# Retention mixer: the sample output in a bank of its own, the sequence steps from the gate units on, and twenty matmuls of the output projection in the last head's tail

## What is computed

```python
def _retention_mixer(h, s0, pos0, w_in, gn_g, w_out):
    p = h @ w_in                                    # q, k (4 heads x 256), v, gate (4 heads x 512)
    q = _rotary(q, pos0);  k = _rotary(k, pos0) * (RET_DK ** -0.5)
    o, s = _retention_chunked(q, k, v, s0)          # per chunk of 128 tokens and head:
    #   att = (q k^T) * decay;  o = att v + (q * q_dec) s;  s = s * s_dec + (k * k_dec)^T v
    o = (o - mu) * lax.rsqrt(var + LN_EPS) * gn_g   # over the 512 values of a head
    o = o.reshape(B, L, RET_VW) * jax.nn.silu(gate)
    return o @ w_out, s

x = _layer_norm(ALPHA * x + (1.0 + gate_m) * y, ln_g[i, 0], ln_b[i, 0])
h = x * (1.0 + scale_f) + shift_f                   # goes to the router and the experts
```

## Time and profile before

| | |
|---|---|
| time, median of 3 runs | 2185.55 us |
| lowest and highest | 2180.12 and 2189.08 us |
| profiled execution: its own time | 2183.24 us |
| profiled execution: span in the trace | 2181.0 us |
| PE busy | 1841.5 us, 84% of the span |
| PE weight loads | 981.8 us |
| DVE, ACT, POOL busy | 788.5, 378.7, 347.4 us |
| `retention`, first to last matmul | 45.5 to 611.5 us |
| `mixer_end` of layer 0, first matmul | 612.15 us |

### The profile page before, as it was taken

The page is one execution under the profiler, slowest core; times in us unless marked ns, Lnnn a source line. Parts: engine busy times, 40 slices in busy tenths (PEclk is TensorE's granted clock), DMA queues, the critical chain, the costliest instruction groups (busy, mean ns, idle before and its releaser), DMA issues. The chain is left out here.

```text
span 2181.0 us, 36947 instructions
## 1 busy us (share of the span) xinstructions
PE 1841.5 (84%) x15665; PEld 981.8 (45%) x15665; DVE 788.5 (36%) x1650; ACT 378.7 (17%) x832; POOL 347.4 (16%) x456
## 2 busy tenths in 40 slices
PE   4999999999799769957979989988987779949970
PEld 3444444444334433324555665755754544433320
DVE  0123223223432320025764555555545423240107
ACT  1000000000000011114332242232232110001212
POOL 0011110101102200022521022031031002120103
PEclk9999999999989879978998989999998789959995
DMA  9364738556260199968431034034033584078964
GB/s 342 125 235 171 262 125 298 191 181 232 98 222 39 69 388 400 397 267 267 130 94 46 11 110 123 12 103 117 18 128 103 181 266 138 20 261 298 401 239 179
DMA packets 235089, 397.44 MB, mean 182 GB/s; under 512 B 17677, under 2 KB 91381, under 8 KB 234870
## 3 DMA queue, kind: packets, MB, share of 16 engines
q1 hardware_dynamic: 228974, 373.58, 49.1%
q0 software_dynamic: 5952, 21.50, 2.6%
HBM read 301.53 MB, written 93.51 MB: 181 GB/s over the span
## 5 line engine op out<-in xcount | busy, mean ns | idle before, releaser
L583 PE MATMUL bank<-ring,hT 128*128 128x512 f32 x768 | 349.7, 607 | 4.1 <-PEq L282 2.2
L583 PEld LDWEIGHTS bank<-ring,hT 128*128 128x128 f32 x768 | 144.7, 193 | 189.1 <-issue 188.9
L1235 PE MATMUL bank<-hT,ring 128*128 128x272 f32 x768 | 218.1, 419 | 0.0
L2385 PE MATMUL bank<-expert_w,exp_xT 128*32 128x512 f32 x1152 | 179.2, 630 | 13.2 <-DMA expert_w<-in_moe_w_gu_dram 9.1
L1235 PEld LDWEIGHTS bank<-hT,ring 128*128 128x128 f32 x768 | 141.2, 197 | 32.8 <-issue 8.0
L3095 PE MATMUL bank<-ring,oT 128*128 128x512 f32 x336 | 151.6, 613 | 0.7 <-PEq L484 0.7
L1229 PE MATMUL bank<-ring,hT 128*128 128x512 f32 x256 | 129.4, 636 | 0.0
L2385 PEld LDWEIGHTS bank<-expert_w,exp_xT 128*32 128x32 f32 x1152 | 48.0, 115 | 125.3 <-issue 120.1
L3095 PEld LDWEIGHTS bank<-ring,oT 128*128 128x128 f32 x336 | 65.6, 196 | 82.6 <-issue 82.6
L2409 PE MATMUL bank<-expert_w,exp_aT 128*32 128x512 f32 x576 | 89.5, 613 | 10.7 <-DMA expert_w<-in_moe_w_down_dram 9.3
L1905 DVE SCALAR_TENSOR_TENSOR dn_y<-dn_pre,dn_conv,dn_y 128x568 f32<-128x568 f32 x96 | 91.1, 949 | 3.4
(11 more groups left out here) (499 smaller groups left out, 2609.8 us busy)
## 6 DMA issues: line engine op xcount, KB each, us to landing
ring<-in_w_ada_dram SPq DMA_DIRECT2D x24, 2048.0 KB, 9.3
expert_w<-in_moe_w_gu_dram SPq DMA_DIRECT2D x24, 2048.0 KB, 15.5
expert_outputs<-ret_zeros SPq DMA_DIRECT2D x15, 2048.0 KB, 9.9
expert_w<-in_moe_w_down_dram SPq DMA_DIRECT2D x24, 1024.0 KB, 16.7
ring<-in_ret_w_in_dram SPq DMA_DIRECT2D x8, 2048.0 KB, 13.8
ret_Ss<-in_state_ret_dram SPq DMA_DIRECT2D x32, 512.0 KB, 5.2
out_dram<-ret_Ss SPq DMA_DIRECT2D x32, 512.0 KB, 4.2
oT<-in_moe_w_gu_dram SPq DMA_DIRECT2D x8, 2048.0 KB, 20.7
```

The lines of the kernel that those rows point to most:

```text
L583: last = pe.matmul(ps[u % 2][:, :], core.hT[:, k, tok(t)], core.ring[:, w % RING, k, :], start=(k == 0), stop=(k == KD - 1))
L1235: mm = pe.matmul(ps[U % 2][:, 0:HALF], core.ring[:, w % RING, k, c * P:(c + 1) * P], core.hT[:, k, half * HALF:(half + 1) * HALF], start=( ...
L2385: last = pe.matmul(ps[v][G * j:G * (j + 1), :], xT[:, v, k, G * j:G * (j + 1)], wgu[of[j] % SLOTS][:, k, :], start=(k == 0), stop=(k == KD ...
```

## The change

- `seq` has bank 5 for the sample output, in which the sample's scores stood. So it needs no turn of bank 6 or 7 and may run between the chunks. `out` in exchange has bank 4 alone.
- The sequence steps stand in a table `MIDDLE`: 0 in round 3, 2 in 5, 3 in 6, 4 in 7, 5 in 8, 6 in 10, 7 in 11. On PE, where the round has a unit, they are put between its fourth and fifth matmul; on the other engines they come ahead of the unit's part. `seq` 1 is behind `norm` 0 in round 4.
- Since `seq` and `chunk` share banks 2 and 3, each now waits for the other's updates on DVE (`st_done` in `seq`, `ss_done` in `chunk`). The att v of the sample moves to the last `seq`.
- `EARLY`: twenty of the 32 matmuls of tile 0 of the output projection, those of heads 0 to 2 (for the second half of the columns only those of heads 0 and 1), are issued in rounds 5 to 11 of the last pass, three in a round (two in the last), behind the round's sequence step and ahead of its other steps; their sums stay open in banks 0 and 1 across the barrier. SP issues the third block of `w_out` in round 5 of the last pass.
- `mixer_end` of layer 0 does the twelve left, in the order tile 0 half 0, tile 1 half 0, tile 0 half 1, tile 1 half 1, and then `route(0)`; from tile 2 on all is as before.

```diff
+EARLY = [(c, k) for c in range(2) for k in range(KD)] + [(0, k) for k in range(KD, KD + 4)]
...
-                 6: [("out", 0), ("chunk", 3), ("norm", 2)], 7: [("seq", 0), ("out", 1), ("norm", 3), ("seq", 1)],
-                 8: [("seq", 2), ("out", 2)], 9: [("seq", 3), ("seq", 4)], 10: [("seq", 5), ("out", 3)],
-                 11: [("seq", 6), ("seq", 7), ("stat", NPT)], 12: [("fold", 4), ("norm", 4)], 13: [("out", 4)]}
-
-        def program(project, step):
+                 6: [("out", 0), ("chunk", 3), ("norm", 2)], 7: [("out", 1), ("norm", 3)], 8: [("out", 2)],
+                 10: [("out", 3)], 11: [("stat", NPT)], 12: [("fold", NPT), ("norm", NPT)], 13: [("out", NPT)]}
+        MIDDLE = {3: [("seq", 0)], 5: [("seq", 2)], 6: [("seq", 3)], 7: [("seq", 4)], 8: [("seq", 5)], 10: [("seq", 6)],
+                  11: [("seq", 7)]}
+        STEPS[4] += [("seq", 1)]
+        early = lambda r: [ck for n, ck in enumerate(EARLY) if n // 3 == r - 5]
+
+        def program(project, step, split=False):
 
             for h in range(H + 1):
                 for r in range(UNITS):
                     u = UNITS * h + r - NT
+                    middle = [(what, h - 1, i) for what, i in MIDDLE.get(r, ()) if h > 0]
+                    whole = not (split and 0 <= u < UNITS * H)
+                    for each in middle if whole else ():
+                        step(*each)
+                    if h == H:
+                        step("early", H - 1, r)
                     if 0 <= u < UNITS * H:
-                        project(u // UNITS, u % UNITS // NT, u % NT, u)
+                        project(u // UNITS, u % UNITS // NT, u % NT, u, *(() if whole else (middle,)))
...
+                    if what == "early" and i == 5:
+                        core.load(sp, core.mix[0][14])
...
-                core.load(sp, core.mix[0][14])
...
+                    if what == "early":
+                        for c, k in early(i):
+                            block = core.mix[0][12 + 2 * (k // KD) + c]
+                            if k == 0:
+                                pe.wait_ge(*taken(UNITS * H - 2 + c))
+                            if k % KD == 0:
+                                pe.wait_ge(*core.arrival(block))
+                            pe.matmul(ps[c][:, :], oT[:, k, tok(0)], core.ring[:, block % RING, k % KD, :],
+                                      start=(k == 0), stop=False)
...
+                        pe.wait_ge(s["ss_done"], 2 * (DECB * h + (1, 1, 3, 4)[i]))
                         o = ps[6 + x % 2]
...
-                        x = o_unit(h, NPT)
-                        o = ps[6 + x % 2]
+                        o = ps[5]
                         if i == 0:
-                            pe.wait_ge(s["o_done"], x - 1)
                             pe.wait_ge(s["qds_done"], h + 1)
+                            pe.wait_ge(s["att_done"], 2 * (h + 1))
+                        if i < 4:
+                            pe.wait_ge(s["st_done"], 2 * (NPT * h + (0, 2, 2, 3)[i]))
+                        if i == 4:
                             pe.wait_ge(s["st_done"], 2 * NPT * (h + 1))
...
-                        if x >= 2:
-                            pe.wait_ge(s["oT_kept"], x - 1)
+                        if x:
+                            pe.wait_ge(s["oT_kept"], x)
...
+                def product(t, c):
+
+                    for k in range(2 * KD):
+                        if t == 0 and k % KD == 0:
+                            weights(2 * (k // KD) + c)
+                        if t == 0 and (c, k) in done:
+                            continue
...
+                if l == 0:
+                    for c in range(2):
+                        for t in range(2):
+                            product(t, c)
+                    route(0)
+                for t in range(0 if l else 2, NT):
...
-                    dve.wait_ge(s["y_done"], 2 * (t + 1))
+                    dve.wait_ge(s["y_done"], 3 if t == 0 and l == 0 else 2 * (t + 1))
```

More of the change, by code:

```diff
@@ L582, in project @@
                             sample_parts(pe, core, ps[(u + 1) % 2], w).then_inc(s["parts_done"], 1)
+                        for each in middle if k == KD // 2 else ():
+                            step(*each)
                         last = pe.matmul(ps[u % 2][:, :], core.hT[:, k, tok(t)], core.ring[:, w % RING, k, :],
@@ L660, in step @@
                     if what == "fold":
-                        x = o_unit(h, NPT)
                         pe.wait_ge(s["spread_done"], h + 1)
-                        pe.matmul(ps[6 + x % 2][:, 2 * P:2 * P + 24], core.fold[:, :], spread[:].rearrange("p j f -> p (j f)"),
+                        pe.matmul(ps[5][:, 2 * P:2 * P + 24], core.fold[:, :], spread[:].rearrange("p j f -> p (j f)"),
                                   start=True, stop=True).then_inc(s["o_ps"], 1)
@@ L3073, in choose @@
                     last.then_inc(s["logits_done"], 1)
-                for t in range(NT):
+                done = () if l else EARLY
+                def product(t, c):
[4 more added lines that the diff above has]
+                            continue
+                        last = pe.matmul(ps[2 * (t % 2) + c][0:rows(t), :], values(t)[:, k, :],
+                                         blocks[2 * (k // KD) + c][:, k % KD, :],
+                                         start=(k == 0), stop=(k == 2 * KD - 1))
+                    last.then_inc(s["y_done"], 1)
+                if l == 0:
[4 more added lines that the diff above has]
+                for t in range(0 if l else 2, NT):
                     if t >= 2:
@@ L3091, in _ @@
                     for c in range(2):
-                        for k in range(2 * KD):
-                            if t == 0 and k % KD == 0:
-                                weights(2 * (k // KD) + c)
-                            last = pe.matmul(ps[2 * (t % 2) + c][0:rows(t), :], values(t)[:, k, :],
-                                             blocks[2 * (k // KD) + c][:, k % KD, :],
-                                             start=(k == 0), stop=(k == 2 * KD - 1))
-                        last.then_inc(s["y_done"], 1)
+                        product(t, c)
                     if t:
```

24 lines of the change are left out of this document (12 added, 12 removed).

## The result

| | before | after |
|---|---|---|
| time, median | 2182.84 us (2178.57 to 2189.08, 4 runs) | 2153.07 us (2149.98 to 2155.34, 4 runs) |
| ratio, 95% interval | | 0.9855 [0.9824, 0.9887] |
| span of the profiled execution | 2181.0 us | 2153.2 us |

The change makes the kernel faster, as forecast, but the 2164.0 us of the forecast are 10.9 too many, and the time is 3 us under the range.

What follows compares the result with a forecast made beforehand. PE was taken as the bound in `retention` and `mixer_end`. Terms: -19.7 + 0.1 (`mixer_end`) + 4.0 + 1.7 (tail) - 3.3 - 2.6 (passes) = -19.8, taken as 2164 us, range 2156 to 2173.

Steps and rivals of the forecast that it cites:

- The base: Whole kernel: -19.8 us gave 2163.4 from the profiled execution's 2183.24, or 2165.8 from the median 2185.55; 2164 was taken.
- Matmuls out of `mixer_end`: Tiles 0 and 1 in `mixer_end`: 19.7 us less, 17.2 for twenty matmuls and 2.5 for the clock.
- The wait for h: PE ahead of `route(0)`: vectors at 24 us, h of tile 0 at 37.9, a wait of 0.1 us (0 to 4.6).
- rival (a): `mixer_end`: the vectors do not come sooner and `route(0)` waits 4.6 us; time 2168, chance 0.17.
- The tail: Last head, chunk 1 to `mixer_end`: 55.8 us, 4.0 more than 51.86, plus one clock drop of 1.7.
- Rival (e): Tail: the early matmuls fill nothing and the gaps stay 15.5 us instead of 9.4; time 2170, chance 0.07.
- Waits of the passes: PE, rounds 3 to 11 of passes 1 to 3: 2.75 us go, 1.65 come, net 3.3 us less.
- Rival (d): Chunks and sequence steps sharing banks 2 and 3 wait for DVE at each step; slower, 2205, chance 0.03.
- Clock of the passes: Passes 1 to 3: drops costing 5.1 us go, half of three new waits cost 1.7 each; net 2.6 less.
- Rival (b): Passes and tail: every wait of 1.65 us drops the clock, 7.7 us more; time 2171, chance 0.10.
- The ring on SP: Modulation block's load, issued later behind sequence steps: 13.5 us for 9.5 to landing, so no wait.
- Rival (c): A modulation block takes 20.2 us instead of 9.5, 13.4 us late over two passes; time 2177, chance 0.05.

Runs made afterwards that it cites:

- e8_fourteen: The changed kernel with fourteen early matmuls, two in a round of the tail, instead of twenty; 2151.49 us, ratio 0.9863.
- e2_early_only: The kernel before with only the early matmuls, the earlier load and the new order of `mixer_end`, sequence steps in their old rounds; 2161.45 us, ratio 0.9915.
- e5_vectors_first: The changed kernel with the residual rows of tiles 1 to 3 and the sample loaded behind the vectors in `mixer_end`; 2150.62 us, ratio 0.9867.
- e1_seq_only: The kernel before with only the sequence steps moved, no early matmuls and `mixer_end` in its old order; 2161.24 us, ratio 0.9906.
- e10_placed: The changed kernel with part of the early matmuls ahead of the sequence step that would wait, the rest behind it; 2152.05 us, ratio 0.9874.
- after again: The changed kernel run again without any edit; 2153.69 us, ratio 0.9889.
- e11_after_third: The changed kernel run once more without any edit, on the chip of the placed kernels; 2158.26 us, ratio 0.9905.
- e6_late_st_wait: The changed kernel with a sequence step's wait for the update of S put behind its 8 small matmuls; 2149.27 us, ratio 0.9856.
- e7_both: The changed kernel with the edits of e5_vectors_first and e6_late_st_wait together; 2153.66 us, ratio 0.9882.
- e9_placed_all: The kernel of e10_placed with the edits of e5_vectors_first and e6_late_st_wait added; 2145.9 us, ratio 0.9847.

## Why the prediction was wrong in its size

**The base.** This is the step that failed: "Against the profiled execution's own 2183.24 that is 2163.4". The sum of the changes was subtracted from one execution, as if the rest behind the routing, which no edit touches, stayed as long as it was there; a median of three, 2185.55, stood beside it. Over all groups, 52 executions of the kernel before average 2178.6 us, with a standard deviation of 5.7 (2167.11 to 2190.7). The profiled one was long in the stretch that no edit touches: 1413.8 us behind the start of the routing, where the twelve other profiled executions of this study have 1399.0 to 1409.3. Between the two profiled executions the span fell by 27.8 us; 18.0 of it stand ahead of the routing and 9.8 in that rest (1403.9 after), for which the forecast had nothing. Of the 14.8 us to the shortest one 10.0 are PE's clock in one stretch of layer 1's mixer, as the windows of the first group show. The same sum of -19.8 from 2178.6 gives 2158.8. That the base was high is not the whole of it: in the forecast's own group the four executions of before average 2183.3 and the four after 2152.9, 30.5 apart with a standard error of 2.8; on the chip of the first group of experiments it is 23.3 (2.0), on that of the third 19.8 (2.0). Why the first is so large stays open. The second fault is the low end: I gave 5.4 us for an execution at the low end of three runs' spread, and the kernel spreads over 24.

**The sum of the terms.** Routing was to start 19.8 us earlier. Measured: mean of before 768.7 (767.25, 770.16), mean of three after 749.0 (749.29, 746.64, 750.98), 19.7 less. The sum is right by luck in part: behind `route(0)` 3.4 us came for which it had nothing, and the passes and the tail gave more than forecast.

**Matmuls out of `mixer_end`**, -19.7 for twenty matmuls and its clock. `route(0)` was reached 17.2 us earlier than before instead of 19.6 (40.26 against 57.48). The 44 matmuls themselves took 38.0 us (608.76 to 646.77, where the wait begins) for the 37.8 of the forecast; the rest is the next term. "If the clock is up" held in this execution; in the two others the stage's first 3 us were at 0.50 and the 44 took 39.6 and 39.5 us, which the wait for h hid in part.

**The wait for h**, forecast 0.1, h at 37.9. Measured: fold 26.38 and h 40.20 us after the first matmul in the profile after, 26.8 and 40.7 in the next one; the wait of PE is 2.25 in the one and 1.10 in the other, which had half-clock matmuls ahead of it. DVE's chain from fold to h was right (13.8). The step that failed is "I take the vectors at 24 us": it took the 4 us of transfers that go with the 2 MB off the fold in full. 4.9 us of DMA work did go, but the engines now start the stage at a share of 0.62 instead of 1.04 and stand idle for 2.6 us before the fold. "Issuing alone, at some 0.45 us each, would be done by 15 us" was wrong too: the rows already showed groups of four at 1.8 us and more, and it takes 20.4 us after the change for 22.2 before. So rival (a) came in by half.

**Behind `route(0)`** the forecast had no term. It cost 3.4 us in all three executions: the small router matmuls (3.08 us for x16 where `route(1)` has 1.96) and the start of tile 2 at the lower clock. This was missed because only waits were looked at and not where the clock would fall. `e8_fourteen` shows that the wait is not needed for it, and `e2_early_only` that the new order of the stage alone doesn't bring it (31.63 us, with the same order). It is 1.7 us in the three kernels that load the vectors first (33.33, 33.32 and 33.32 us), and 3.3 to 3.4 in the other six executions with both halves of the change. The stage's start doesn't decide it: `e5_vectors_first` and `e8_fourteen` begin the stage at 604.97 and 604.94. What sets it remains open. The 0.7 us less up to the routing are a wait: before, one drop of the clock of 1.7 us stood in tile 3 and PE later waited 0.56 us for DVE's `end_momq`; after, the drop stands in the sample's matmuls and covers that wait.

**The tail**, forecast 55.9 (54.2 and one drop of the clock). Measured 55.49 with a drop (the early matmuls at 563.93 take 4.16 us instead of 2.84), 53.84 and 53.85 without. The waits stand at `seq` 1, 2, 3 and 4 and nowhere else, 1.50, 0.93, 1.50 and 1.50 us for 1.65, 0.94, 1.65 and 1.65. Rival (e) falls: against the tail with no early matmuls (`e1_seq_only`, 44.55) twenty of 0.86, 17.2 us, add 9.3 to 10.9. They cost less than their length, and the waits they left could be filled as well (`e10_placed`).

**Waits of the passes**, forecast -3.3. Nine waits of 8.3 us are now three of 4.5, -3.8; the new one is 1.50 and not 1.65. Rival (d) falls: each pass has one wait, at the step with no unit around it, and no unit waits in its middle.

**Clock of the passes**, forecast -2.6, with half of three new waits followed by a drop. The interval between the new waits of two passes is 135.89 us without a drop and 137.60 with one. In the executions after and after again none of three was followed by one, in the third two of three. Chunk 1 is at 553.27, 551.80 and 556.07, against 556.0 in the forecast; the 1.47 us between the first two stand ahead of the first of these waits already. The windows behind the first two of these waits in `e11_after_third` (length, PE busy, clock, DMA share, GB/s) show the one and the other:

```profile
157.00:175.00 18.00, 17.99 (x70) 0.91 0.57 192
```

```profile
294.00:312.00 18.00, 17.40 (x73) 1.00 0.64 208
```

Over the seven executions with three waits of 1.50 (after, again, third, `e1_seq_only`, `e5_vectors_first`, `e8_fourteen`, `e10_placed`) six of twenty-one were followed by a drop, each 1.7 us. Of the nine waits of 0.93 in `e6_late_st_wait`, `e7_both` and `e9_placed_all` none was, of the three of 0.94 in the kernel before one; that shorter waits are safer isn't shown by so few. The Trainium skill, "TensorE: Matmul & The Clock Gate", Part 1, says of the rise of the clock at a kernel's start that it is run-variable; these runs bear on falls and not on that rise. Of the falls behind these waits the runs show something like it: one program had 3.4 us of it in one execution and none in two. Rival (b) falls.

**The ring on SP**, no wait forecast. The load of the modulation block is issued at 351.84 in the profile after and used at 365.91, 14.1 us later for the 13.5 of the forecast, and PE has no wait for it. Rival (c) falls.

What stays open is 3 us: from 2178.6, 19.7 less is 2158.9, and the fourteen executions of the changed kernel average 2155.6 (standard deviation 3.5). Their profiled stretches behind the routing, 1403.9 to 1406.5, lie inside the 1399.0 and 1413.8 of the two of before. On the chip of the third group the difference of the means is 19.8 (2178.1 against 2158.3). The 23.1 us between the averages have a standard error of 1.2, and the 19.7 rest on two and three profiled executions that spread over 2.9 and 4.3 us. So this can be chance of executions and chips; that the later stages gain something of their own isn't shown or excluded. The idle time of PE for which the profile names no releaser does stand elsewhere in them: ahead of the modulation products 10.9 and 7.6 us before, 0.6 to 1.0 after, ahead of `dn_X,dn_T` 3.6 and 4.1 before, 6.8 to 7.4 after.

## What to carry to other kernels

Take the base of a forecast from more than one execution: compare the stretch that the change leaves alone, and give the range at least the spread that the same program shows there. When a stage loses matmuls ahead of its first use of loaded vectors, lay out both what is ahead of them: the issues on the queue, at their durations in the trace, and the transfers, with the time in which the DMA engines will now be empty at the stage's start. A matmul that can be issued early belongs between a producer's last matmul and the first instruction that waits for the answer, not behind the pair; and two edits that fill the same gaps don't add.

## What the runs showed of the hardware

- Loads on SP's queue took 0.6 us each when issued one behind another (34 in 20.4 us, 24 of them of 32 KB and nine of 512 KB), though single ones show 0.43; behind a block of 2 MB that is still under way, four of 512 KB took 4.18 us instead of 2.11.
- An idle time of 1.50 us on PE was followed by a drop of the granted clock in six of twenty-one cases, at the same place of the same program in some executions and not in others; each cost 1.7 us. Behind the first transposes of `mixer_end` the lower clock cost 0, 1.7 or 3.4 us from kernel to kernel, and 3.4 in all three executions of the changed one; what sets it is not known.
- Two executions of one unchanged program differed by 14.8 us in a stretch of 1400 us. 10.0 of it stood in one stretch of 71 to 81 us with the same work and the same idle time, where the granted clock was 1.00 in the one and 0.86 in the other.
